# Hybrid attention and retention layer on 8 cores: the normalised input of the main part comes transposed from DRAM and is scaled by GpSimd

## The reference, cut to what matters

```python
D_MODEL = 1024; BATCH = 4; SEQ = 8192; DEPTH = 1
h = rmsnorm(x, norm_g[l])                       # x * rsqrt(mean(x*x) + eps) * g, per token
proj = jnp.einsum('bsd,de->bse', h, w_in[l])    # 1024 -> 2816 columns
aq, ak, av, az, rq, rk, rv, rz = jnp.split(proj, cuts, axis=-1)
a = sliding_window_attention(aq, ak, av, att_sinks[l]) * jax.nn.silu(az)   # window 128, blocks of 128
r = retention(rq, rk, rv, ret_gn_g[l]) * jax.nn.silu(rz)                   # chunks of 128, state carried on
mix = jnp.concatenate([a, r], axis=-1)
x = x + jnp.einsum('bse,ed->bsd', mix, w_out[l])
return rmsnorm(x, final_g)
```

## Time and profile before

| | |
|---|---|
| median of 3 runs | 715.12 us (714.89 to 715.48) |
| the profiled execution, its own time | 716.18 us |
| its span, first to last instruction (slowest core, core 6) | 714.7 us |
| spans of the eight cores | 708.3 to 714.7 us |
| PE busy | 631.4 us, 88% |
| DVE busy | 572.5 us, 80% |
| ACT busy | 425.1 us, 59% |
| POOL busy | 197.1 us, 28% |
| DMA, prefix (slices 1 to 8) | 203 to 338 GB/s |
| DMA, main part | about 75 GB/s |

### The profile page before, as it was taken

The page is one execution under the profiler, slowest core; times in us unless marked ns, Lnnn a source line. Parts: engine busy times, 40 slices in busy tenths (PEclk is TensorE's granted clock), DMA queues, the critical chain, the costliest instruction groups (busy, mean ns, idle before and its releaser), DMA issues.

```text
span 714.7 us, 17246 instructions; the slowest of 8 cores (708.3 to 714.7 us)
## 1 busy us (share of the span) xinstructions
PE 631.4 (88%) x5555; PEld 391.1 (55%) x5555; DVE 572.5 (80%) x1219; ACT 425.1 (59%) x748; POOL 197.1 (28%) x254
## 2 busy tenths in 40 slices
PE   0596786988998999999999999999999999999984
PEld 0364554555565555656665656555555565555551
DVE  0687887557898898888888788878998888988885
ACT  3677667544656556666665646566455656555552
POOL 2734243101223223222323122321222222222321
PEclk9989999899999999999999999999999999999998
DMA  8999979600222222222222222222222222200002
GB/s 243 328 338 289 309 220 318 203 16 2 74 75 74 75 76 75 75 75 75 75 75 76 75 75 76 74 75 75 75 74 75 76 74 76 75 31 31 32 30 89
DMA packets 23847, 77.76 MB, mean 109 GB/s; under 512 B 3152, under 2 KB 3536, under 8 KB 23760
## 3 DMA queue, kind: packets, MB, share of 16 engines
q1 hardware_dynamic: 23760, 76.67, 32.0%
HBM read 59.88 MB, written 16.78 MB: 107 GB/s over the span
## 4 chain that ended last, share of the span: by engine, by line
PE 77%; DVE 9%; issue 5%; DMA 3%; ACT 3%; POOL 2%; SPq 0%; DVEq 0%; POOLq 0%; ACTq 0%
PE ps L690 36%; PE ps L1010 13%; PE ps L696 10%; PE ps L683 4%; PE ps L930 3%; PE ps L886 2%; PE ps L999 2%; PE ps L853 2%; DMA dkt<-dk_pre 2%; DVE gg L988 1%; DMA wstage<-w_r 1%; DVE yy L1014 1%; POOL stat L672 1%; DVE hh L520 1%; DVE Sst L919 1%
## 5 line engine op out<-in xcount | busy, mean ns | idle before, releaser
L690 PE MATMUL ps<-Wa,hT 128*128 128x512 bf16 (+2 forms) x1032 | 167.4, 316 | 9.5 <-ACT hT L504 5.7
L690 PEld LDWEIGHTS ps<-Wa,hT 128*128 128x128 bf16 x1032 | 88.7, 99 | 66.7 <-issue 10.2
L1010 PE MATMUL ps<-Wo,mixT 128*128 128x512 bf16 x512 | 116.2, 380 | 6.3 <-ACT mixT L504 3.6
L690 PE MATMUL ps<-Wb,hT 128*128 128x512 bf16 x512 | 115.7, 379 | 0.0
L672 POOL TENSOR_TENSOR stat<-stat,neghalf 128x1 f32<-128x1 f32 x64 | 37.3, 590 | 201.9 <-DVE stat L669 200.8
L862 POOL TENSOR_SCALAR_AFFINE_SELECT PT<-PT 128x1024 bf16<-128x1024 bf16 x63 | 74.8, 1187 | 61.0 <-ACT PT L856 59.1
L986 POOL TENSOR_TENSOR gns<-gns,neghalf 128x4 f32<-128x4 f32 x32 | 35.3, 1104 | 186.7 <-DVE gns L983 158.8
L1010 PEld LDWEIGHTS ps<-Wo,mixT 128*128 128x128 bf16 x512 | 48.0, 98 | 65.8 <-issue 13.1
L690 PEld LDWEIGHTS ps<-Wb,hT 128*128 128x128 bf16 x512 | 48.8, 98 | 53.1
L813 ACT ACTIVATE gate<-ps 128x512 f32<-128x512 f32 x64 | 38.1, 595 | 57.4 <-PE ps L690 30.4
L856 ACT ACTIVATE PT<-ps,negC 128x1024 bf16<-128x1024 f32 x64 | 70.9, 1109 | 1.0 <-PE ps L853 0.6
(11 more groups left out here) (127 smaller groups left out, 1147.8 us busy)
## 6 DMA issues: line engine op xcount, KB each, us to landing
xs<-x_all SPq DMA_DIRECT2D x64, 512.0 KB, 7.8
out<-yy SPq DMA_DIRECT2D x32, 512.0 KB, 3.0
wstage<-w_r SPq DMA_DIRECT2D x16, 640.0 KB, 9.4
tb<-tabs SPq DMA_DIRECT2D x32, 256.0 KB, 4.4
wstage<-w_o SPq DMA_DIRECT2D x8, 512.0 KB, 8.3
wstage<-w_k SPq DMA_DIRECT2D x2, 512.0 KB, 6.4
gate<-cs_pre SPq DMA_DIRECT2D x2, 512.0 KB, 12.8
fg_rep_s<-fg_rep SPq DMA_DIRECT2D x1, 512.0 KB, 7.3
```

What stands on the lines that cost most here:

```text
L690: S.add("pe", lambda e, kb=kb: e.matmul(bank[:, c0:c0 + n], lhsT=hT[c % 2][:, kb * 128:(kb + 1) * 128], rhs=W[:, kb, w0:w0 + n], start=(kb ...
L1010: S.add("pe", lambda e, kb=kb, bank=bank, half=half: e.matmul(bank[:, 0:512], lhsT=mixT[s2][:, kb * 128:(kb + 1) * 128], rhs=Wo[:, kb, hal ...
```

## The change

For main chunks, T no longer uses PE. The host gives a second copy of the main part of x, `x_t`, laid out so that a chunk's 128 partitions are features and its columns 8 blocks of 128 tokens. A new stage `xload` (offset -3, so chunk t+3 in step t) loads the chunk's 512 KB into a staging tile `wstage`, shared with the weights. The token scales, one number in each of 128 partitions of `stat`, are stored to a row of a DRAM tensor (`rs_scr`, queue names rw0, rw1) and loaded back as a row repeated in all partitions (`rrow`, queue names rr0, rr1), both issued by SP; the load waits until the store has landed. POOL then multiplies the staged chunk with the row and writes `hT`. The scaling to `hh` and the copy out of PSUM are gone for main chunks. The store of the output becomes a stage of its own, a step later in the program than before. The rule for urgency changes for a DMA that another DMA waits for. The prefix is computed as before.

```diff
-    order=[("load", -9, -4), ("tload", -3, -4), ("GF", 2, None), ("M", None, 2), ("PV", None, 1),
+    order=[("store", None, 3), ("load", -9, -4), ("tload", -3, -4), ("xload", None, -3), ("GF", 2, None), ("M", None, 2), ("PV", None, 1),
...
             for d in o.deps:
-                if o.urg < d.urg:
-                    d.urg = o.urg
+                u = o.urg + 250 if o.eng == "sp" and d.eng == "sp" else o.urg
+                if u < d.urg:
+                    d.urg = u
...
+    xT_d = dram("x_t", [NM * CH, D], F32)
+    rs_d = nc.dram_tensor("rs_scr", [NM, CH], F32, kind="Internal").ap()
...
-        S.add(scale_rows(hh[hx(c)][:], xs[sx][:], stat[st][:, 2:3], D,
-                         engines=(opts["hscale_main"] if is_main(c) else opts["hscale_pre"])),
+        if is_main(c):
+            m = c - NP
+            S.add("sp", dma(rs_d[m:m + 1, :].rearrange("o p -> p o"), stat[st][:, 2:3]), reads=[b_stat[st]],
+                  writes=[b_rs[m % 4]], dmaq=f"rw{m % 2}")
+            S.add("sp", dma(rrow[m % 2][:], rs_d[m:m + 1, :].to_broadcast([128, CH])), reads=[b_rs[m % 4]],
+                  writes=[b_rrow[m % 2]], dmaq=f"rr{m % 2}")
+            return
+        S.add(scale_rows(hh[hx(c)][:], xs[sx][:], stat[st][:, 2:3], D, engines=opts["hscale_pre"]),
...
+    def st_xload(c):
+        m = c - NP
+        st_t, b_st, q = stage_slot()
+        xT_slot[c] = (st_t, b_st)
+        S.add("sp", dma(st_t[:, 0:D], xT_d[m * CH:(m + 1) * CH, :]), writes=[b_st], dmaq=q)
...
     def st_T(c):
+        if is_main(c):
+            st_t, b_st = xT_slot[c]
+            m = c - NP
+            i0 = st_t[:, 0:D].rearrange("p (k t) -> p k t", k=8)
+            o = hT[c % 2][:].rearrange("p (k t) -> p k t", k=8)
+            i1 = rrow[m % 2][:].unsqueeze(1).to_broadcast([128, 8, CH])
+            S.add({e: (lambda e: e.tensor_tensor(out=o, in0=i0, in1=i1, op=ALU.mult)) for e in T_ENG},
+                  reads=[b_st, b_rrow[m % 2]], writes=[b_hT[c % 2]], cost={"pool": 1.9, "dve": 1.25})
+            return
...
-        S.add("sp", dma(out_d[m * CH:(m + 1) * CH, :], yy[s2][:]), reads=[b_yy[s2]], dmaq=f"st{s2}")
+
+    def st_store(c):
+        s2, m = c % 2, c - NP
+        S.add("sp", dma(out_d[m * CH:(m + 1) * CH, :], yy[s2][:]), reads=[b_yy[s2]], dmaq=f"st{s2}")
```

More of the change, by code:

```diff
@@ L26 @@
 SCHEDULE = True
+T_ENG = ("pool",)
 DEFAULT_OPTS = dict(
     pools={"A": [0, 1, 2, 7], "B": [3, 4, 5, 6]},
-    order=[("load", -9, -4), ("tload", -3, -4), ("GF", 2, None), ("M", None, 2), ("PV", None, 1),
+    order=[("store", None, 3), ("load", -9, -4), ("tload", -3, -4), ("xload", None, -3), ("GF", 2, None), ("M", None, 2), ("PV", None, 1),
            ("OR", None, 1), ("KV", None, 1), ("O", None, 2), ("G", 1, None), ("R", None, 0), ("SC", None, 0),
@@ L446, in build_program @@
     den, b_den = slots("den", 2, [128, 16], F32)
-    tmpa, b_tmpa = slots("tmpa", 1, [128, 512], F32)
     gns, b_gns = slots("gns", 2, [128, 12], F32)
@@ L462, in build_program @@
     b_Gbf, b_GT = b_yy
+    rrow, b_rrow = slots("rrow", 2, [128, CH], F32)
+    b_rs = [Buf(f"c_rs{i}") for i in range(4)]
     stat2, b_stat2 = slots("stat2", 2, [128, 4], F32)
@@ L482, in alloc_pair @@
         return ps_all[:, i * 512:(i + 2) * 512], [b_bank[i], b_bank[i + 1]]
-    qnames = ["pe", "act", "dve", "pool", "const", "constB", "cs0", "cs1", "dkt"]
+    qnames = ["pe", "act", "dve", "pool", "const", "constB", "cs0", "cs1", "dkt", "rw0", "rw1", "rr0", "rr1"]
     qnames += [f"ws{i}" for i in range(NST)]
@@ L1040, in run_stage @@
             st_front(c)
+        elif name == "xload":
+            if main:
+                st_xload(c)
         elif name == "T":
@@ L1078, in run_stage @@
             st_O(c)
+        elif name == "store":
+            st_store(c)
     order = opts["order"]
     t_first = min(o for n, o, m in order if o is not None)
-    for t in range(t_first, NT + 3):
+    for t in range(t_first, NT + 4):
         if t == t_first:
@@ L1205, in _core_inputs @@
     d["tabs"] = _const_tables(pos0[NP:])
+    d["x_t"] = np.ascontiguousarray(main.reshape(NM, CH, 8, 128).transpose(0, 3, 2, 1)).reshape(NM * CH, D)
     d["masks"] = masks.astype(ml_dtypes.bfloat16)
```

1 line of the change is left out of this document (added).

## The result

The changed kernel takes 1279.03 us (median of 4 runs, 1276.52 to 1282.5), the kernel before 715.3 beside it (714.89 to 715.8): 1.789 times the time, with a 95% interval of 1.785 to 1.793. The forecast was 695.0, with a range from 681 to 709. The cores' spans lie between 1255.6 and 1279.1 us, so no single core is to blame.

The account below looks back on a forecast made before the run. The prediction took PE to bound the main part. It summed -13.6 (transposes) - 11.5 (waits for `hh`) + 5 (start) = -20.1 us, from 716.18 to 696.1, or 695.0 us on the median's scale; range 681 to 709.

Parts of the forecast that it names:

- GpSimd's multiplication: On POOL, after the power and two DMAs of 1.7 us each: `hT` ready over a step early, PE pays nothing.
- its cover: Time in hand before POOL's masks are needed for PV; said to be gone if both DMAs take over 12 us together.
- Behind the load of the row on SP stand ..., cost nothing: SP's queue in the main part: output store, later loads and next `x_t` have at least most of a step; cost nothing.
- The transposes, -13.6 us: On PE in the main part: 31 groups of eight transposes at 0.44 us each go for certain, 13.6 us saved.
- The waits for `hh`, -11.5 us: PE's 13 waits at the first transpose of `hh` in the main part go with the transposes, 11.5 us saved.
- the second rival: Main part: DVE late as before, PE waits elsewhere, only streaming time won: 706.5 us, or 711.5 with a slower start; chance 0.23.
- GpSimd's product: POOL's multiplication of the 128 x 1024 chunk in each main step: 1.9 us, POOL at 6.5 of some 16.7 us.
- the third rival: Main part: POOL's product blocks DVE's instructions that read SBUF, step 19.0 us, +48 us, or 763; chance 0.09.
- The start, +5 us: Start of the main part: `hT` of chunk 32 at 131 to 134 instead of 128.1 us; +5 us, bounds 2 and 10.

Follow-up runs that it names:

- a1: Changed kernel without issuing the store and load of the scales; the product takes a row of ones, scaling by token left out: 720.39 us.
- a2: Changed kernel with the store's pieces 512 bytes apart and the load reading a row of another tensor, scaling by token left out: 764.01 us.
- a6: Changed kernel with only the load's source changed to a row of another tensor, scaling by token left out: 1044.36 us.
- a4: Changed kernel with store and load issued, but the product takes a constant row and does not wait for the load: 991.58 us.
- b2: a1 with one wait for each queue instead of one for each producer, all lists the same: 735.5 us.
- b1: a1 with GpSimd's product cut to one eighth, 128 x 128 elements, the rest of `hT` not renewed: 705.84 us.
- f3: b1 with the planner's handicap against VectorE, for copies ScalarE could do as well, at 1.0 instead of 0.4 us: 697.52 us.
- c2: Changed kernel, complete, with the row of scales made by a TensorE matmul instead of through DRAM, and one wait for each queue: 714.51 us.
- a3: Changed kernel, complete, with each engine waiting once for each queue, only for the last of several producers: 1147.29 us.
- c3: c2 with the product on VectorE, reading the row straight from PSUM without the copy: 722.12 us.

## Why the prediction was wrong

*The step that failed* is in the part on GpSimd's multiplication: "Store and load of the row come next, 1.7 us each if they take what a small DMA takes on an empty queue". The row used, of a 32 KB load, prices a DMA that moves data in large pieces; the new store writes 128 pieces of 4 bytes into one stretch of 512 bytes. It measured 6.8 to 18.7 us, the load of the row just written 5 to 16 us; a1, a2 and a6 settle that this is the cause. The text named the point from which its cover is gone, "if the two DMAs take over 12 us together", and it was right there: together they take 21 to 25 us in most steps. But no duration that reaches this point was ever used: it was 1.7 us each in the main part, and at its start 6 to 9 us for the store, because of large loads ahead of it. Nor was it asked what happens beyond the point, where GpSimd's list closes into a loop. It should have been a rival with a chance of its own, and its price a loop of some 36 us a step, since the planner's list on GpSimd has `gns`, the masks and the next power behind the product.

The Trainium skill (DMA: Bandwidth & Descriptors, Specifications), which the prediction cited, says that below 512 B the DMA does a read-modify-write. No run here shows the read-modify-write itself. The pieces of a2's store are below 512 B as well, and it is through in 1.6 us by the median when no two share 512 bytes; what the runs add is that as many pieces on one stretch take ten times as long. The prediction put the sentence aside as "hidden like the rest", which the store was not.

*"Behind the load of the row on SP stand ..., cost nothing"*: wrong with the same term. SP waited 318.7 us for the store, and a4 shows 271 us lost even when the product does not wait for the row.

*The transposes, -13.6 us*: a step in which PE waits for nothing takes 16.73 us before (five of them) and 16.28 us in b2 (six), so the streaming time of 0.44 us is real. It shows in the time only where the waits let it. *The waits for `hh`, -11.5 us*: wrong in the planner's own lists. They reappear at the scores as the waits of b1 for `Sst` and `mix`, 10.1 us in 475; b1, which has no trip and hardly a product, comes to 705.8, and the second rival ("the wait only moves") had said 706.5. The forecast had counted with the copies of `aqT` and `rv` that the planner gives back to VectorE, and still expected these waits to go. Where more copies are kept away from VectorE (f3), they do, and 697.5 is reached. From 185 to 660 us, the kernel before, b1 and f3 (columns as above; the third pair is VectorE):

```profile
185.00:660.00 475.00, 456.25 (x4110) 277.54 (x4108) 407.46 (x879) 288.82 (x529) 125.14 (x136) 1.00 0.21 73
```
```profile
185.00:660.00 475.00, 455.71 (x3959) 277.80 (x4013) 406.09 (x882) 267.51 (x511) 139.95 (x166) 0.99 0.31 103
```
```profile
185.00:660.00 475.00, 465.99 (x4104) 281.07 (x4103) 382.48 (x827) 307.44 (x594) 146.00 (x169) 1.00 0.30 103
```

VectorE is as busy in b1 as before.

*GpSimd's product*: 2.34 to 2.39 us, not 1.9, and the third rival's mechanism is real. It named the final scaling and the products of `gate`, and both occur (b2, a1). It costs 14.6 us in a1's lists (a1 against b1) and 29.7 in b2's, less than the 48 it was priced at: in a1 it holds up VectorE in 9 of 27 steps. In the earlier trace rows, from which it was read, the scaling's record starts 0.04 us ahead of the mask's, so those rows alone do not tell who has to wait. The prediction also read the rule of the Trainium skill (SBUF — State Buffer, Who interferes with whom) too narrowly: that an instruction with one input in SBUF does not contend holds there only outside the two-port modes. The same section adds that casts, copies and `tensor_scalar` can take both port pairs in a two-port mode, and whoever comes first keeps them for its whole instruction. The trace agrees: in c2 a cast with one SBUF input took 2.47 instead of 0.28 us, and a `tensor_scalar` on 128 x 4 elements 2.35 instead of 0.16 when it started 0.03 us behind the product; 0.03 us ahead of it (448.95) it took its 0.16.

*The start, +5 us*: without the trip the first main projections come at 132.1 us instead of 128.1 (a1), so +4.0 for the wait on `x_t` and the product; with it at 146.4, as the first store takes 16.5 and the load 6.6 us.

*Not foreseen at all*: the 84 waits in a row on GpSimd, 132 us by a3. Before, ScalarE or VectorE wrote `hT`, and these wait for PE all along; GpSimd, which does so only here, has all the readers of `hT` still ahead of it (argued from the counts, 2767 and 239).

What stays open: how a4's 271 us divide between SP's late loads and other queues. PE stood with "issue" in the middle of a projection at 726 us for 7.6 us, while SP's issue of `xs<-x_all` took 8.3 us; that both come from queues clogged by the two small DMAs is argued, not shown. How far apart the pieces must lie was tried at 512 bytes only. Nor was it tried to keep the whole way through DRAM with the store spread and the row gathered from there. And why the handicap brings 19 to 20 us in a1 and c3 was only shown as a sum of loads, not step by step.

## What to carry to other kernels

Price a DMA by the pieces that it writes and where they fall, not by its bytes: a column of 128 scales stored into one row of 512 bytes, and read back at once, cost 559 of 1279 us here with all that followed from it, and a matmul with a unit matrix gives the same row without it. If a new hop has no row in the profile, follow what is queued behind its consumer, and write down what a step costs if the hop is ten times the guess. And when work is moved to GpSimd, what counts is where in VectorE's stream it falls: the same 2.4 us cost 3 or 30 us, and the gain of a shorter TensorE stream showed only once VectorE had been given slack.

## What the runs showed of the hardware

- 128 four-byte writes to one 512-byte stretch of DRAM: 6.8 to 18.7 us until the next dependent DMA could be issued (changed kernel); to 128 stretches: 1.6 us by the median (a2). A load of 128 copies of one 512-byte row: 3.1 to 3.6 us by the median if the row is old (a2, a6), 5 to 16 if just written this way.
- Waits that no longer wait for anything are not free in number: 84 of them took 5.3 us on GpSimd, 0.06 us each, where the records show 17 ns for one.
- A product of 128 x 1024 f32 on GpSimd with a row repeated by the access pattern takes 2.34 to 2.39 us by the mean of a run's 32; with a column repeated it took 1.89 the one time it occurs.
- Some VectorE instructions that start within such a product last until it ends, whatever their size: products of two tiles in SBUF (2.83 instead of 0.69 us, a1), a cast of `Sst` (2.47 instead of 0.28, c2) and a `tensor_scalar` on 128 x 4 elements (2.35 instead of 0.16, c2). Those with one operand in PSUM are not touched: in a1 `yy<-ps,xs` starts within a product 30 times and takes 0.68 to 0.69 us, as always.
- In the changed kernel's main part, where PE idled for 40% of the time, its granted clock was 0.72 on average, and its own work took longer: 627.6 us for some 30 steps without transposes, against 472.5 us for 28 steps with them before.
